# The down projection of a two-block layer as seven block products, with the next norm begun inside the last

## The chip, the cores and the metric

One core of one Trainium2 chip. The metric is the device time of the whole kernel in microseconds, the median of repeated runs of the same program with the same inputs (batch 1, 1024 tokens, width 1024, float32).

## The reference, cut to what matters

Two layers follow each other: a block with retention, forgetting attention and a gated feed-forward part, then a block with latent and dilated attention. The change touches the last product of the first block and the first norm of the second:

```python
h2 = rmsnorm(x, g_ffn)                                   # (1024, 1024)
ff = (silu(h2 @ w_gate) * (h2 @ w_up)) @ w_down          # hidden width D_FF = 2816 = 22 * 128
x = x + ff
# second block
h = rmsnorm_2(x, attn_norm_g)
proj = h @ w_in                                          # begins with c_q, c_kv, k_rope: 416 columns
```

All products must come out in near-float32 precision, so every operand is split.

## The kernel before

**Splitting.** Each operand `a` of a product is split into `ah` (rounded, by a copy) and `al = a - ah`, and a product is three matmuls, `ah bh + ah bl + al bh`, each of a 128x128 stationary tile and 512 moving columns, accumulated in a PSUM bank.

**Weights.** SyncE loads the weights of nearly all stages in units of 128x512 (256 KB) into the two slots of `raw` (L4131), in one long loop; GpSimd turns each unit into `wh` and `wl` (L4154, L4156) once the slot's last user has begun the next one. The eight units of the latent projection get tiles of their own (L2975, L2977), and GpSimd begins them when the down projection's splits stand at 18 of the second half's 22 (`COVERED`).

**The stage before.** `FeedForward` makes the hidden tensor: tile by tile, 22 tiles of 128 features by 1024 tokens. Its weights go through `up_raw`. Tiles 2 to 21 leave a two-slot staging area for `ff_dram` and come back into `FF` (11 MB in SBUF) by five loads (`BACK`, L2536) on ScalarE's DMA queue: the first (3 MB) while the last tiles are made, the other four (2, 1.5, 1.5 and 2 MB) at once after the last tile.

**`Down`.** `X += FF^T w_down`, in two halves `c` of 512 output columns. For each half it runs over the 22 feature tiles; per tile ScalarE copies it to `fh` (L2791, L2795, L2802, L2810), VectorE subtracts (`fl`, L2831, L2837, L2847, L2852), and TensorE does 8 token tiles x 3 matmuls of `fh`/`fl` with the unit's `wh`/`wl` (L2895), in all eight PSUM banks. That is 2 x 22 x 8 x 3 = 1056 matmuls. The four 1 MB loads of `X` from `x_dram` (L2813) are issued one per two tiles in the midst of the first half. VectorE adds the banks to `X` (L2859) after each half. The last two tiles of the second half (L2876) run staggered, so that the third norm begins beside them: squares and roots on ScalarE (L544, L570), scaling on VectorE (L613), transposes on TensorE (L667), a copy (L516) and a subtraction (L619) into `hth` and `htl`, the split operand of what follows. The norm does all of its token tiles in one order, with the transposes of tiles 0 and 1 inside the last product and those of tiles 2 and 3 behind it.

**The stage after.** `Latent` (L335) takes tokens 0 to 511 over eight 416-column units, with the transposes of tiles 4 to 7 between them, then tokens 512 to 1023.

Each engine runs its own list in program order. Lists are written out by hand; a wait stops all that stands behind it on its engine.

## Time and profile before

| | |
|---|---|
| median of 3 runs | 2978.2 us (2977.5 to 2980.61) |
| the profiled execution | 2988.91 us, its span 2987.1 us |
| mean granted TensorE clock | 0.983 |
| busy: TensorE, its weight loads | 2880.0 us, 2311.1 us |
| busy: VectorE, ScalarE, GpSimd | 1801.3 us, 1146.4 us, 823.0 us |
| DMA | 251.63 MB, 84 GB/s in the mean |

The profiled execution is 10.7 us longer than the median; all times of the trace are its own. The profile gives for each engine its busy time, and for each group of instructions what ended the idle time before it. Recorded matmuls overlap, so the time of one is read from the distance of starts, not from its duration. Times in the views below are microseconds from the start of the span.

### The profile page before, as it was taken

The numbers are of one execution on the slowest core, as the hardware profiler recorded it, in microseconds if no ns is written. First come the engines' busy times: TensorE is split into PE (matmuls) and PEld (weight loads), VectorE is DVE, ScalarE is ACT, GpSimd is POOL, SyncE is SP. The second block draws the span as 40 slices with busy tenths as digits, with TensorE's granted clock in tenths as the row PEclk, the third lists the DMA queues.
The fourth block names the chain that finished last, engine by engine and source line by source line (L and its number), as shares of the span: only waits on it lengthen the run. The fifth ranks groups of instructions, "written<-read, shape, count | busy, mean of one in ns | idle before, by whom it ended". The sixth has DMA issues, their size and how long they took to land.

```text
span 2987.1 us, 37403 instructions
## 1 busy us (share of the span) xinstructions
PE 2880.0 (96%) x14042; PEld 2311.1 (77%) x14042; DVE 1801.3 (60%) x2313; ACT 1146.4 (38%) x1908; POOL 823.0 (28%) x581
## 2 busy tenths in 40 slices
PE   7999999899999999999999999999999999999998
PEld 6778777678877888887888766668788888877886
DVE  2583666675587665554436488850566565686568
ACT  2232555433034333321223366641445444444313
POOL 2414110311532000004443600014344343440253
PEclk8999999999999999999999999999999999999999
DMA  3102000224433222225113300013323323223452
GB/s 131 39 22 83 18 22 22 74 85 151 169 120 116 99 85 71 78 102 186 60 46 112 99 8 15 22 41 103 95 74 82 80 72 82 68 78 113 155 192 97
DMA packets 112536, 251.63 MB, mean 84 GB/s; under 512 B 13441, under 2 KB 26497, under 8 KB 108289
## 3 DMA queue, kind: packets, MB, share of 16 engines
q1 hardware_dynamic: 64736, 131.91, 13.7%
q10 hardware_dynamic: 47648, 117.62, 11.7%
q8 instruction: 106, 1.74, 0.2%
q14 instruction: 46, 0.37, 0.0%
HBM read 184.48 MB, written 52.43 MB: 79 GB/s over the span
## 4 chain that ended last, share of the span: by engine, by line
PE 77%; DVE 13%; ACT 4%; issue 2%; POOL 1%; DMA 1%; ACTq 1%; POOLq 0%; SPq 0%; DVEq 0%
PE ps L390 13%; PE ps L2773 13%; PE ps L335 8%; PE ps L2895 8%; PE ps L1972 7%; PE ps L2002 6%; PE ps L2360 3%; PE ps L1172 3%; PE ps L1214 1%; PE ps L1189 1%; PE ps L3111 1%; PE ps L1191 1%; PE ps L3368 1%; PE ps L1190 1%; PE ps L374 1%
## 5 line engine op out<-in xcount | busy, mean ns | idle before, releaser
L4154 POOL TENSOR_TENSOR wh<-raw,zeros 128x512 fp32r<-128x512 f32 x276 | 324.8, 1177 | 2120.1 <-DMA raw<-in_stream_dram 627.2
L4156 POOL TENSOR_TENSOR wl<-raw,wh 128x512 fp32r<-128x512 f32 x276 | 463.0, 1677 | 21.7
L390 PE MATMUL ps<-hth,wh 128*128 128x512 f32 x704 | 286.3, 407 | 2.1 <-DVE fox_vl L1396 2.1
L390 PE MATMUL ps<-hth,wl 128*128 128x512 f32 x704 | 280.4, 398 | 0.0
L390 PE MATMUL ps<-htl,wh 128*128 128x512 f32 x704 | 280.1, 398 | 0.0
L2831 DVE TENSOR_TENSOR htl<-ff,hth 128x1024 fp32r<-128x1024 f32 x40 | 82.4, 2060 | 139.8 <-ACT hth L2802 71.0
L390 PEld LDWEIGHTS ps<-htl,wh 128*128 128x128 f32 x704 | 133.3, 189 | 32.4
L390 PEld LDWEIGHTS ps<-hth,wh 128*128 128x128 f32 x704 | 133.4, 189 | 31.9 <-issue 2.5
L390 PEld LDWEIGHTS ps<-hth,wl 128*128 128x128 f32 x704 | 133.8, 190 | 26.1
L2895 PE MATMUL ps<-wh,hth 128*128 128x512 f32 x336 | 133.0, 396 | 0.5 <-DVE htl L2837 0.5
L2895 PE MATMUL ps<-wh,htl 128*128 128x512 f32 x336 | 132.9, 396 | 0.0
L2895 PE MATMUL ps<-wl,hth 128*128 128x512 f32 x336 | 132.9, 395 | 0.0
L335 PE MATMUL ps<-wh,hth 128*128 128x512 f32 (+1 forms) x320 | 123.4, 386 | 4.5 <-POOL wl L4156 1.6
L2773 PE MATMUL ps<-htl,up_wh 128*128 128x512 f32 x320 | 126.1, 394 | 0.0
L2773 PE MATMUL ps<-hth,up_wh 128*128 128x512 f32 x320 | 126.1, 394 | 0.0
L2773 PE MATMUL ps<-hth,up_wl 128*128 128x512 f32 x320 | 126.1, 394 | 0.0
L1106 ACT ACTIVATE ps<-ps 128x512 f32<-128x512 f32 x224 | 122.8, 548 | 0.0
L335 PE MATMUL ps<-wl,hth 128*128 128x512 f32 (+1 forms) x320 | 121.7, 380 | 0.0
L335 PE MATMUL ps<-wh,htl 128*128 128x512 f32 (+1 forms) x320 | 121.3, 379 | 0.0
L1105 ACT ACTIVATE mla_pth<-ps 128x512 fp32r<-128x512 f32 x128 | 76.3, 596 | 80.4 <-PE ps L1172 78.9
L2540 ACT ACTIVATE up_wh<-up_sums 128x512 fp32r<-128x512 f32 x80 | 50.1, 631 | 143.9 <-PE ps L2773 133.0
L2002 PE MATMUL ps<-merge_oth,wh 128*128 128x512 f32 x256 | 102.1, 399 | 0.0
(603 smaller groups left out, 7691.5 us busy)
## 6 DMA issues: line engine op xcount, KB each, us to landing
raw<-in_stream_dram SPq DMA_DIRECT2D x284, 256.0 KB, 2.6
up_raw<-in_stream_dram SPq DMA_DIRECT2D x21, 1024.0 KB, 5.7
merge_raw<-in_stream_dram SPq DMA_DIRECT2D x12, 1024.0 KB, 7.1
merge_sg_dram<-merge_sg ACTq DMA_DIRECT2D x12, 1024.0 KB, 5.7
merge_sg<-merge_sg_dram ACTq DMA_DIRECT2D x12, 1024.0 KB, 4.9
dil_stg<-dil_stg ACTq DMA_DIRECT2D x96, 128.0 KB, 2.4
ff_dram<-ff SPq DMA_DIRECT2D x20, 512.0 KB, 3.0
merge_m<-in_stream_dram ACTq DMA_DIRECT2D x6, 1024.0 KB, 5.3
```

What stands on the lines that cost most here:

```text
L335: ins = nc.tensor.matmul(ps[:, t, 0:n], a[:, k, P * t:P * t + P], b[:, slot(j), c:c + n], start=first and q == 0, stop=final and q == 2)
L390: ins = nc.tensor.matmul(ps[:, bank + half, :], w[:, j, c:c + P], a[:, k, HALF * half:HALF * half + HALF], start=k == 0 and q == 0, stop=k ...
L1106: a.did(nc.scalar.activation(self.scores(g), self.scores(g), ACT.Exp, scale=self.scale), f"p{g}")
L1172: ins = nc.tensor.matmul(self.scores(g), m, r, start=q == 0, stop=q == len(pairs) - 1)
L1972: ins = nc.tensor.matmul(self.made(i, k), w[:, n, P * kt:P * kt + P], m[x][:, kt, :], start=begins and kt == 0 and q == 0, stop=kt == 3 an ...
L2002: ins = nc.tensor.matmul(ps[:, bank + half, :], w[:, br, P * k:P * k + P], x[:, 4 * br + k, HALF * half:HALF * half + HALF], start=n == 0 ...
L2360: ins = nc.tensor.matmul(ps[:, bank + t, :], xh[:, j, P * t:P * t + P], w, start=begins and q == 0, stop=ends and q == 2, skip_group_check ...
L2773: ins = nc.tensor.matmul(self.made(i, k), w[:, n, P * kt:P * kt + P], m[x][:, kt, :], start=begins and kt == 0 and q == 0, stop=kt == 3 an ...
L2831: nc.vector.tensor_tensor(self.fl[:, s, :], self.ff.FF[:, bass.ds(2 * i + s, 1), :].rearrange("p a b -> p (a b)"), self.fh[:, s, :], ALU.s ...
L2895: ins = nc.tensor.matmul(ps[:, t, :], a[:, s, P * t:P * t + P], b[:, s, :], start=first and q == 0, stop=final and q == 2)
L4154: nc.gpsimd.tensor_tensor(wh[:, s, :], raw[:, s, :], zeros[:].to_broadcast([P, HALF]), ALU.add).then_inc(w_hi, 1)
L4156: nc.gpsimd.tensor_tensor(wl[:, s, :], raw[:, s, :], wh[:, s, :], ALU.subtract).then_inc(w_split, 1)
```

## The change

The hidden tensor and the weights are taken as two by two blocks: P, Q (tokens 0 to 511, first and second half of the features) and R, S (tokens 512 to 1023), each of 11 feature tiles; the weights E, F (first half of the features by two column halves) and G, H. Seven products of blocks (11 feature tiles, 4 token tiles, 512 columns, 3 matmuls: 132 each) in this order, with S1 = R + S, S2 = S1 - P, S3 = S - R (all as `x_sum` or `s3`), S4 = Q - S2, and sums T of weight blocks (`w_sum`): `E_P`, `T_S1`, `T_S2`, `G_Q`, `T_S3`, `H_S4`, `T_S`. Each product runs in six steps, one tile and then five pairs of tiles; step n is product n // 6, step n % 6 of it; a full step is 24 matmuls. Products alternate between PSUM banks 4 to 7 and 0 to 3; two pairs of products are accumulated in one bank, and results are added to up to two places of `X`.

Weights no longer pass through the units of `raw` and GpSimd. SyncE loads them as 128x1024 (512 KB) into three slots, 48 loads in all since the sums read blocks again (two per step in `T_S1`); ScalarE copies (`weight_high`) and VectorE subtracts (`weight_low`) into a ring of three places in `wh`/`wl` and free parts of `hth`/`htl`; the hidden tiles have a ring of two (`hidden_high`, `hidden_low`). All sums are made on VectorE, in place, one step ahead. The four loads of `X` are issued right behind those of `FF`. The third norm takes tokens 0 to 511 inside the last product (squares after step 34, roots after 38; transposes of tile 0 after step 38, of 1 and 2 inside 39 and 40, of 3 after 40). GpSimd begins the latent units when all splits of `Down` are done. The core of the diff, `...` where lines are left out:

```diff
@@ class Down @@
+            ADDS = (((0, 0),), ((0, 1), (1, 1)), ((0, 1),), ((0, 0),), ((1, 1),), ((0, 1),), ((1, 0),))
...
+            def raw_released(self, eng, m):
+                if m < 6:
+                    eng.wait_ge(self.w_low, m + 1)
+                elif m < 18:
+                    eng.wait_ge(self.w_sums, (m - 6) // 2 + 1)
...
+            def weight_high(self, act, n):
+                k, g = divmod(n, self.GROUPS)
+                if n in (1, 2):
+                    self.ff.p.wait(act, f"u2x4.{PAIRED - 1}")
+                elif n:
+                    self.group_done(act, n - 3)
...
+                nc.scalar.activation(self.w_ring(n)[0], self.w_source(k, g), ACT.Copy).then_inc(self.w_high, 1)
+
+            def hidden_high(self, act, n):
...
+                    self.group_done(act, n - 2)
...
+            def first_highs(self, act):
+                self.weight_high(act, 0)
+                self.ff.v.wait(act, f"ff1.{PAIRED - 2}")
+                self.hidden_high(act, 0)
+                self.hidden_high(act, 1)
 
             def act(self, act, norm):
+                self.weight_high(act, 1)
                 self.ff.v.wait(act, f"ff2.{PAIRED - 1}")
...
                 for n in range(1, len(self.ff.BACK)):
                     self.ff.load_back(act, n)
...
+                for t in range(0, NT, 2):
+                    act.dma_start(self.X[:, t:t + 2, :], self.x_dram[:, t:t + 2, :]).then_inc(self.loaded, 16)
+                for n in range(2, self.LAST + 1):
+                    self.weight_high(act, n)
...
+                    self.hidden_high(act, n)
+                    if n == 34:
...
+                        norm.load(act)
+                        for t in range(4):
+                            norm.late_square(act, self.summed, t, 0)
+                    elif n == 38:
+                        norm.late_warm(act)
+                        for t in range(4):
+                            norm.late_root(act, self.summed, t)
...
+            def sums(self, dve, n):
...
+                if k == self.T_S1:
...
+                    self.x_sum(dve, R_, R_, S_, ALU.add)
+                    e = self.load_no(k, g, True)
+                    self.raw_loaded(dve, e - 1)
+                    self.raw_loaded(dve, e)
+                    self.w_sum(dve, T, raw, self.raw(e, g))
+                elif k == self.T_S2:
+                    dve.wait_ge(self.x_sums, g + 1)
+                    self.x_sum(dve, R_, R_, P_, ALU.subtract)
+                    self.raw_loaded(dve, self.load_no(k, g))
+                    dve.wait_ge(self.w_sums, g + 1)
+                    self.w_sum(dve, T, raw, T)
...
             def dve(self, dve, norm):
...
+                for n in range(2, self.LAST + 1):
+                    k, g = divmod(n, self.GROUPS)
+                    if n == 38:
+                        norm.late_base(dve, 0)
+                        for t in range(4):
+                            self.add(dve, self.H_S4, t)
+                    if n < self.LAST:
+                        self.sums(dve, n + 1)
+                    if k == self.T_S2:
+                        self.s3(dve, g)
+                    self.weight_low(dve, n)
...
+                    self.hidden_low(dve, n)
+                    if 0 < k < 6 and 2 <= g:
+                        self.add(dve, k - 1, g - 2)
+                    if n == 39:
+                        norm.scaled(dve, 0)
+                        norm.scaled(dve, 1)
...
+                    pe.wait_ge(self.w_low, n + 1)
+                    pe.wait_ge(self.x_low, n + 1)
+                    for j in range(self.size(g)):
+                        for t in (2, 3, 1, 0) if n == 0 else range(4):
+                            if g == 0:
+                                self.accumulator_free(pe, k, t)
+                            for q, (a, b) in enumerate(((xh, bh), (xh, bl), (xl, bh))):
+                                ins = nc.tensor.matmul(ps[:, self.BANK[k] + t, :], a[:, j, P * t:P * t + P], b[:, j, :], start=fresh and g == 0 and q == 0,
...
@@ class Latent @@
-                pool.wait_ge(down.hi, FT + self.COVERED)
-                pool.wait_ge(down.lo, FT + self.COVERED)
+                down.split_through(pool)
```

## Rows read from the trace of the kernel before

**Rows 1.** The page: busy time, share of the span, instructions of TensorE.

```profile
PE 2880.0 (96%) x14042; PEld 2311.1 (77%) x14042; DVE 1801.3 (60%) x2313; ACT 1146.4 (38%) x1908; POOL 823.0 (28%) x581
```

**Rows 2.** Stretches, the whole stage: us, busy time (count) by engine, PEclk, DMA share, GB/s.

```profile
1344.46:1602.39 257.93, 252.12 (x1090) 202.31 (x1088) 111.57 (x77) 61.00 (x84) 117.07 (x100) 0.99 0.30 102
```

**Rows 3.** Groups of instructions, 1344.46 to 1602.39: count | busy us, mean ns | idle before.

```profile
L2895 PE MATMUL ps<-wh,hth 128*128 128x512 f32 x336 | 133.0, 396 | 0.5 <-DVE htl L2837 0.5
L2831 DVE TENSOR_TENSOR htl<-ff,hth 128x1024 fp32r<-128x1024 f32 x40 | 82.4, 2060 | 139.8 <-ACT hth L2802 71.0 <-ACT hth L2810 68.9
L2810 ACT ACTIVATE hth<-ff 128x1024 fp32r<-128x1024 f32 x20 | 21.2, 1060 | 88.3 <-PE ps L2895 88.3
L2859 DVE TENSOR_TENSOR down_x<-down_x,ps 128x512 f32<-128x512 f32 x14 | 8.9, 678 | 1.0 <-PE ps L2876 1.0
L2975 POOL TENSOR_TENSOR lat_wh<-raw,zeros 128x416 fp32r<-128x416 f32 x7 | 8.6, 1230 | 1.8 <-DMA raw<-in_stream_dram 1.8
L667 PE MATMUL ps<-ident,norm_xn 128*128 128x128 f32 x32 | 5.1, 313 | 3.6 <-DVE norm_xn L613 3.6
```

**Rows 4.** Timeline of TensorE's weight loads: start us, us, engine, line, operands.

```profile
1330.17 0.19 PEld L2773 LDWEIGHTS ps<-up_x2h,up_wl 128*128 128x128 f32 x1
...
1335.61 0.19 PEld L2773 LDWEIGHTS ps<-up_x3h,up_wl 128*128 128x128 f32 x1
...
1569.89 0.19 PEld L2895 LDWEIGHTS ps<-wh,hth 128*128 128x128 f32 x1
...
1576.89 0.19 PEld L2895 LDWEIGHTS ps<-wh,hth 128*128 128x128 f32 x1
```

**Rows 5.** Timeline of TensorE, 1602 to 1611, same columns, idle time before in brackets.

```profile
1602.39 0.71 PE L335 MATMUL ps<-lat_wh,hth 128*128 128x416 f32 x1 [1.41 <-DVE htl L619]
1606.72 1.76 PE L667 MATMUL ps<-ident,norm_xn 128*128 128x128 f32 x8
1610.57 1.03 PE L667 MATMUL ps<-ident,norm_xn 128*128 128x128 f32 x8
```

**Rows 6.** Stretches elsewhere, columns as in rows 2.

```profile
855.00:865.00 10.00, 8.18 (x29) 6.28 (x28) 9.80 (x8) 2.12 (x3) 4.25 (x2) 0.83 0.46 173
1350.00:1360.00 10.00, 9.53 (x41) 7.36 (x41) 4.41 (x3) 2.12 (x2) 4.66 (x4) 1.00 1.01 392
1600.00:1610.00 10.00, 8.59 (x34) 7.87 (x33) 8.30 (x13) 5.16 (x13) 5.60 (x5) 0.59 0.48 158
```

**Rows 7.** Timeline of VectorE at both ends of the stage.

```profile
1349.64 1.23 DVE L2837 TENSOR_TENSOR htl<-ff,hth 128x1024 fp32r<-128x1024 f32 x1 [1.18 <-ACT hth L2795]
1590.69 1.28 DVE L613 SCALAR_TENSOR_TENSOR norm_xn<-down_x,norm_r,norm_g 128x1024 f32<-128x1024 f32 x1
1592.49 1.28 DVE L619 TENSOR_TENSOR htl<-ps,hth 128x512 fp32r<-128x512 f32 x2
```

**Rows 8.** Timeline of ScalarE's sequencer after the last hidden tile.

```profile
1348.63 2.02 ACTq L2536 DMA_DIRECT2D ff<-ff_dram  x4
```

**Rows 9.** Instructions of line 2813: ns min/median/max, first and last start us.

```profile
L2813 ACTq DMA_DIRECT2D down_x<-x_dram x4: 326/332/339, 1385.4 to 1418.9; - x4
```

**Rows 10.** DMA issues in 1350.1 to 1351: count, KB, us from issue to landing.

```profile
ff<-ff_dram ACTq DMA_DIRECT2D x1, 2048.0 KB, 23.1
```

**Rows 11.** DMA queues in 1357 to 1360: packets, MB, share of 16 engines.

```profile
q10 hardware_dynamic: 240, 0.96, 79.9%
q1 hardware_dynamic: 140, 0.26, 22.5%
```

**Rows 12.** DMA issues in 1348–1352, 1352–1357, 1367–1371, 1580–1583.

```profile
raw<-in_stream_dram SPq DMA_DIRECT2D x1, 256.0 KB, 2.7
raw<-in_stream_dram SPq DMA_DIRECT2D x1, 256.0 KB, 6.8
raw<-in_stream_dram SPq DMA_DIRECT2D x1, 256.0 KB, 3.1
norm_g<-in_attn_norm_g_dram ACTq DMA_DIRECT2D x1, 512.0 KB, 3.8
```

More of the change, by code:

```diff
@@ L2777, in build_two_blocks @@
         class Down:
-            TRANSPOSES = {4: 0, 6: 1}
+            E_P, T_S1, T_S2, G_Q, T_S3, H_S4, T_S = range(7)
+            GROUPS, LAST = 6, 7 * 6 - 1
+            BANK = (4, 0, 4, 0, 4, 0, 4)
+            FRESH = (0, 1, 3, 5)
+            ADDS = (((0, 0),), ((0, 1), (1, 1)), ((0, 1),), ((0, 0),), ((1, 1),), ((0, 1),), ((1, 0),))
             def __init__(self, scope, ff, x_dram):
                 self.ff, self.x_dram = ff, x_dram
-                self.fh, self.fl = hth[:, 4:6, :], htl[:, 4:6, :]
@@ new lines, in __init__ @@
+                self.raw_slots = (own[:], htl_f[:, 5:7, 0:HALF], htl_f[:, 3:5, 0:HALF])
+                self.raw_in = [sem(f"down_raw_in{n}") for n in range(3)]
+                self.x_sums, self.s3_made, self.w_sums = sem("down_x_sums"), sem("down_s3_made"), sem("down_w_sums")
+                self.x_high, self.w_high = sem("down_x_high"), sem("down_w_high")
+                self.x_low, self.w_low = sem("down_x_low"), sem("down_w_low")
+                self.done, self.full, self.added = sem("down_done"), sem("down_full"), sem("down_added")
@@ new lines, in raw, with raw_loaded, x_source, w_source @@
+            def raw(self, m, g):
+                return self.raw_slots[m % 3][:, 0:self.size(g), :]
+            def raw_loaded(self, eng, m):
+                eng.wait_ge(self.raw_in[m % 3], 16 * (m // 3 + 1))
+            def x_source(self, k, g):
+                return self.hidden(*((0, 0), (1, 0), (1, 0), (0, 1), (0, 0), (0, 1), (1, 1))[k], g)
+            def w_source(self, k, g):
+                if k in (self.T_S1, self.T_S2):
+                    return self.kept(g)
+                if k == self.T_S:
+                    return self.last_sum(g)
+                return self.raw(self.load_no(k, g), g)
@@ new lines, in added_at, with sp, load @@
+            def added_at(self, k, t):
+                return 4 * sum(len(x) for x in self.ADDS[:k]) + len(self.ADDS[k]) * (t + 1)
+            def sp(self, sp):
+                def load(m, half, c, g):
+                    if m in (1, 2):
+                        self.ff.p.wait(sp, f"g2c.{PAIRED - 1}")
+                    elif m:
+                        self.raw_released(sp, m - 3)
+                    sp.dma_start(self.raw(m, g), self.weights(half, c, g)).then_inc(self.raw_in[m % 3], 16)
+                for g in range(self.GROUPS):
+                    load(self.load_no(self.E_P, g), 0, 0, g)
+                for g in range(self.GROUPS):
+                    load(self.load_no(self.T_S1, g), 0, 1, g)
+                    load(self.load_no(self.T_S1, g, True), 0, 0, g)
+                for k, half, c in ((self.T_S2, 1, 1), (self.G_Q, 1, 0), (self.T_S3, 0, 0), (self.H_S4, 1, 1), (self.T_S, 1, 0)):
+                    for g in range(self.GROUPS):
+                        load(self.load_no(k, g), half, c, g)
@@ new lines, in weight_high @@
+            def weight_high(self, act, n):
[4 more added lines that the diff above has]
+                    self.group_done(act, n - 3)
+                if k in (self.E_P, self.G_Q, self.H_S4):
+                    self.raw_loaded(act, self.load_no(k, g))
+                else:
+                    act.wait_ge(self.w_sums, {self.T_S1: 0, self.T_S2: 6, self.T_S3: 12, self.T_S: 18}[k] + g + 1)
+                nc.scalar.activation(self.w_ring(n)[0], self.w_source(k, g), ACT.Copy).then_inc(self.w_high, 1)
@@ new lines, in hidden_high @@
+            def hidden_high(self, act, n):
+                k, g = divmod(n, self.GROUPS)
+                if n < 2:
+                    self.ff.p.wait(act, f"s4d.{PAIRED - 1}")
+                else:
+                    self.group_done(act, n - 2)
+                if k == self.E_P and g:
+                    act.wait_ge(self.ff.back[0 if g < 4 else 1], 16)
+                elif k == self.T_S3:
+                    act.wait_ge(self.s3_made, g + 1)
+                elif k in (self.T_S1, self.T_S2, self.H_S4):
+                    act.wait_ge(self.x_sums, {self.T_S1: 0, self.T_S2: 6, self.H_S4: 12}[k] + g + 1)
+                nc.scalar.activation(self.x_ring(n)[0], self.x_source(k, g), ACT.Copy).then_inc(self.x_high, 1)
```

358 lines of the change are left out of this document (195 added, 163 removed).

## The prediction

> **What bounds the kernel now.** First the page: TensorE is busy 96% of the 2987.1 us span, so the first question is how many matmuls go and at what price [rows 1]. Then the stretch that the change rewrites, from the first weight load of the down projection to the first matmul of the latent projection: 257.93 us, TensorE busy for 252.12, the granted clock 0.99, VectorE busy for only 111.57 [rows 2]. The groups of that stretch show who has room: the matmuls of L2895 (three groups of 336, of which one stands) wait 0.5 us in all, and 48 of L2876 close the product; VectorE's splits take 2060 ns each, with 139.8 us of idle time before them; half of ScalarE's copies take 1060 ns with 88.3 us before them [rows 3]. So this stage is bound by TensorE, and VectorE has some 146 us free. The period of one matmul is not its recorded 396 ns (they overlap): thirty weight loads lie between 1569.89 and 1576.89, so 0.2333 us each; in the stage before, with operands in other tiles, 24 took 5.44 us, 0.2267 each [rows 4].
>
> The budget closes: 1056 x 0.2333 = 246.4, four transposed tiles 5.1, idle time 0.5 + 3.6 + 1.4 before them and before the latent projection, together 257.0 of 257.9 [rows 2 to 5]. The clock stands at 0.59 in 1600 to 1610, after those idle times, that is partly at 1.2 instead of 2.4 GHz: the latent projection's first twelve matmuls and the eight transposes behind them take until 1608.5, 6.1 us; at full clock that is twelve of 0.19 (estimated from the tile, 416/512 of 0.2333) and 1.03, 3.3. That loses 2.8 us [rows 5, 6].
>
> **Matmuls removed.** Seven products of 11 x 4 x 3 = 132 are 924 against 1056: 132 x 0.2333 = 30.8 us less, 215.6 left. The splits' operands now sit in `wh` and `hth`, as at L2895, so I take 0.2333; at 0.2267 it were 6.1 us less again. Four tiles' transposes stay, 4 x 1.03 = 4.1 [rows 4, 5].
>
> **VectorE's price.** The splits of 128x1024 cost 2060 ns, but one outside GpSimd's weight splits took 1.23 us [rows 3, 7]. The change takes GpSimd out of this stage. Recorded times overlap too: two of 128x512, 0.68 each, end after 1.28, so the second costs 0.60; the same 0.09 off 1.23 leaves 1.14 for 128x1024 [rows 3, 7]. Per full step (24 matmuls, 5.6 us) VectorE does: in E_P and G_Q 2 instructions, in T_S3, H_S4 and T_S 3, in T_S1 4, in T_S2 5; adds of 0.6 come on top in the last four steps of each product. T_S1: 4 x 1.14 + 0.6 = 5.2, just under 5.6. T_S2: 5 x 1.14 + 2 x 0.6 = 6.9 in three steps, over by 1.3 each; with 1.3 in the small step and 0.1 in the next, 5.3 over. What VectorE can be ahead is little, because the ring for the hidden tile has two places: its copy starts when step n-2 is done, and 1.06 + 1.14 + 0.3 of hand-overs later the split is ready, 2.9 us before its turn. 5.3 - 2.9 = **2.4 us** of stall. ScalarE has 2 x 1.06 of 5.6 and covers that.
>
> **ScalarE's queue at the start.** Once the hidden tile 19 is made, ScalarE issues four loads of `FF` and, new, at once four of `X`, and only then copies for step 2. Four issues took 2.02 us; an `X` load occupies the sequencer 0.33, 0.45 with what lies between as I estimate, so about 3.9 us from 1348.6 [rows 8, 9]. Then come two copies and a split: 1352.5 + 2 x 1.06 + 1.14 + 0.2 = 1356.0, while step 1 ends at 1344.7 + 36 x 0.2333 = 1353.1. **3.0 us** (bounds 1 and 5: issues that cost nothing extra, or 1 us each). Before, the next copy was needed only at a step whose operands were there.
>
> **The weights' loads behind the burst.** Before, weights came in units of 256 KB, 2.7 us each, 6.8 while `FF` came back [rows 12]; they were asked for 11 us ahead and nobody waited. `FF`'s four loads landed one behind the other, the last 23.1 us after its issue at 1350.2, so at 1373.3, with the DMA engines at 1.01 and 392 GB/s [rows 6, 10]. The 4 MB of `X`, issued from 1385 to 1419 before [rows 9], now follow directly: another 10 to 13 us, so the burst lasts to about 1385. Within it, 140 packets of the weights' queue (128 carry a unit) ran in 1357 to 1360 beside 240 of ScalarE's: some 2.6 us per 256 KB, and 6.8 - 2.6 = 4.2 before the first [rows 11, 12]. Now follow the chain. T_S1 needs two loads per step. Those of its first step are released by the splits of steps 3 and 4, queue behind a 512 KB load that the split of step 2 releases at 1355, and land by 1355 + 4.2 + 4 x 2.6 = 1370, so step 5 just starts in time (1372.9). The loads of its second step wait for the split of step 5 (1371.6), are 512 KB each, and VectorE is to form that sum before it splits for the first step: 1371.6 + 4.2 + 4 x 2.6 = 1386.2, one sum of 1.14, two small splits of 0.6: step 6 starts at 1388.6, and step 5 ended at 1378.5. **10.0 us**. The load that the sum of step 8 needs is released by the sum of step 7 (1387.3), lands 4 us later behind its forerunner (512 KB outside a burst: 3.8 [rows 12]), then 3 x 1.14: 1395.0 against 1391.4, **3.6 us**. From there each sum has its load in 4 us of a 5.6 us step, and the stall ends. Bounds of the two together: 1 us (no burst: two loads in 5.4 us fit) and 16.
>
> A rule bears on this. The Trainium skill (DMA: Bandwidth & Descriptors, Queues, rings and completion order) says that each DMA engine takes turns between the queues that have work, packet by packet. The trace shows 140 against 240 packets, not even turns [rows 11]. By even turns the weights, with packets half as large, would get a third of the bandwidth, 1 MB in some 8 us instead of 10.4, and the time would be 2956.
>
> **The last product.** Tile 1's transposes wait for its scaling, which VectorE does behind the splits of step 39, whose copies stand behind four roots on ScalarE: **1.2 us**, estimated from 1.28 us for a scaling without GpSimd [rows 7] (bounds 0 and 4). The first four tiles then need nothing more at the end: the idle 3.6 and 1.4 us go [rows 3, 5], and the latent projection begins at full clock, 2.8 us saved. GpSimd starts its eight latent units only after the last split, but that is about 11 us before the end (two full steps less 2.6, two tiles' transposes), and a unit costs two instructions of 1.23 [rows 3], as much as its first twelve matmuls: covered; without that cover the latent projection would wait 3 us for its first unit. SyncE's loads for them stand behind the product's last weight load, which a sum releases some two steps before the end, early enough for the first two units. The latent stage's other half (tiles 4 to 7) is ordered as before.
>
> **Clock.** TensorE was idle for 1.8 us of 855 to 865, and the clock's mean fell to 0.83 there [rows 6], a loss of 1.7 us. The stall of 3 us is followed by one that absorbs a slow step, and so is that of 10 us. I count **1.0 us** (bounds 0 and 8, each stall followed by 1.7).
>
> **Sum.** 215.6 + 4.1 + 2.4 + 3.0 + 13.6 + 1.2 + 1.0 = 240.9 instead of 257.9: 17.0, and 2.8 from the clock, 19.8 us less. The profiled execution took 2988.9; 2969.1 after. The median of the three runs lies 10.7 lower, 2978.2, so the forecast is 2958.4, say **2959**.
>
> **Rivals.** (A) The weights are not late: the queue keeps its own pace, or the sums find their loads there. Then T_S1 costs 1 instead of 13.6: 2946; with 0.2267 per matmul 2940. For it: a load issued in 1367 to 1371, while `FF`'s last one was still under way, landed in 3.1 us. Against: the 6.8 in its midst [rows 12]. (B) Slower: VectorE's instructions keep the 2060 ns [rows 3], because not GpSimd but the tiles or the DMA writes make them slow. Then T_S1 takes 5.5 x 4 x 2.06 + 2.6 = 48 instead of 30.8, T_S2 62, the three products of three instructions about 37 each, some 65 us of stall beyond the sum less 5 that the burst hides: 3019. It decides from about 1.5 us per instruction: T_S1 and T_S2 hold 49.5 of them, and 19.8/49.5 = 0.4 above 1.14. Against it: the 1.23, measured while `FF`'s loads began [rows 7]. (C) The stalls bring the clock down each time, and VectorE's gaps are 0.1 larger than I took: 7 + 5 more, 2971. (D) The change saves nothing that can be told, since A's opposite and C come together (issues of 1 us, +2; the burst at 16, +2.4; C's 12): 2976.
>
> **How the numbers follow.** Forecast (2950 to 2966) 0.50; A 0.24; C 0.14; D 0.07; B 0.05. What this kernel's measurement can tell from no change is about 0.2%, 6 us. So faster 0.87, the same 0.07, slower 0.06. The range takes in A to its lower matmul price and C and D: 2940 to 2976.
>
> **What would show it.** Right: 924 matmuls at 0.233; no GpSimd in the stage; VectorE's 128x1024 at 1.2 us; TensorE waiting once about 3 us behind a ScalarE copy, then about 10 and 4 behind VectorE's splits while VectorE itself waits for a weights' DMA; short waits in T_S2; no idle between the last product and the latent projection. Wrong: a gain of over 30 us says that the burst doesn't reach the weights; VectorE at 2 us says B; a latent projection that waits for GpSimd says that its start is not covered.

## The result

| | before | changed | ratio, 95% interval |
|---|---|---|---|
| median, four runs each | 2979.14 us (2977.5 to 2980.61) | 2958.84 us (2954.28 to 2966.69) | 0.9919 (0.9903 to 0.9935) |
| profiled execution, its span | 2988.91 us, 2987.1 us | 2966.69 us, 2964.8 us | |
| first Down matmul to first latent matmul | 257.7 us | 238.1 us | |
| from there to the end | 1384.7 us | 1380.4 us | |

The change makes the kernel 20.3 us faster; 19.8 was forecast, 2959. The total is right and its terms are not: three of them miss by 8.5, 8.6 and 3.9 us, in both directions, and cancel. (In the profiled executions the stage goes from 1344.69 to 1602.39 of 2987.1 before, and from 1346.32 to 1584.43 of 2964.8 after. The forecast counted it from the first weight load, 0.2 us earlier.)

The page's line on TensorE and the stage as one stretch, which answer to [rows 1, 2]; the columns are the same:

```profile
PE 2845.7 (96%) x13910; PEld 2284.8 (77%) x13910; DVE 1856.8 (63%) x2418; ACT 1178.5 (40%) x1948; POOL 723.6 (24%) x493
```

```profile
1346.32:1584.43 238.11, 219.88 (x957) 178.29 (x956) 170.09 (x181) 91.99 (x124) 5.85 (x6) 0.97 0.43 156
```

132 matmuls are gone from the kernel (13910 for 14042). But where TensorE was busy for all but 5.8 us of the stage, it now stands still for 18.2, GpSimd has left the stage, and VectorE works 170 us instead of 112. The groups say who the new waits are owed to, and that VectorE's price is the one that was forecast ([rows 3] had 2060 ns):

```profile
L3100 PE MATMUL ps<-hth 128*128 128x512 f32 x224 | 89.3, 399 | 15.8 <-DVE htl L2960 15.7
L2960 DVE TENSOR_TENSOR htl<-ff,hth 128x1024 fp32r<-128x1024 f32 x35 | 42.7, 1221 | 33.7 <-ACT hth L2894 33.7
L3100 PE MATMUL ps<-wh,hth 128*128 128x512 f32 x84 | 33.5, 399 | 2.5 <-DVE wl L2954 1.3 <-DVE htl L2960 1.2
```

L2954 and L2960 are the splits of weights and hidden tile, L3100 is the matmul. TensorE's timeline places these waits (idle time before in brackets): before step 2, step 6, step 7, and twice in `T_S2`, before steps 15 and 16. A first matmul behind a wait that is recorded at 0.76 instead of 0.47 us is at half clock (1.2 instead of 2.4 GHz).

```profile
1366.12 0.76 PE L3100 MATMUL ps<-hth 128*128 128x512 f32 x1 [11.37 <-DVE htl L2960]
...
1391.33 0.47 PE L3100 MATMUL ps<-wh,hth 128*128 128x512 f32 x1 [1.27 <-DVE wl L2954]
...
1397.64 0.77 PE L3100 MATMUL ps<-hth 128*128 128x512 f32 x1 [3.28 <-DVE htl L2960]
...
1441.70 0.47 PE L3100 MATMUL ps<-wh,hth 128*128 128x512 f32 x1 [1.18 <-DVE htl L2960]
...
1448.57 0.47 PE L3100 MATMUL ps<-hth 128*128 128x512 f32 x1 [1.04 <-DVE htl L2960]
```

**The wait of 11.4 us.** It stands where the prediction put one of 3.0, behind VectorE and ScalarE. ScalarE's timeline, its sequencer as ACTq:

```profile
1350.13 2.15 ACTq L2498 DMA_DIRECT2D ff<-ff_dram  x4
1352.30 10.12 ACTq L2909 DMA_DIRECT2D down_x<-x_dram  x4
1362.53 1.06 ACT L2880 ACTIVATE hth<-htl_f 128x1024 fp32r<-128x1024 f32 x1 [14.89 <-issue]
```

`FF`'s four loads are issued in 2.15 us, as before. The four of `X` behind them take 10.12 us, the first alone 6.50 (1352.30 to 1358.80), the others 1.07 to 1.25; before the change one took 0.33 [rows 9]. The sequencer stands in the DMA instruction itself, and the copy for step 2 stands behind it: "issue" is idle time for which the profile shows no releaser, and here it is the mark of the trouble.

**The waits at steps 6 and 7.** VectorE's timeline there (L2975 is `w_sum`, L2972 `x_sum`):

```profile
1380.56 1.22 DVE L2954 TENSOR_TENSOR htl<-htl_f,hth 128x1024 fp32r<-128x1024 f32 x1
1381.69 1.22 DVE L2960 TENSOR_TENSOR htl<-ff,hth 128x1024 fp32r<-128x1024 f32 x1
1382.83 1.22 DVE L2972 TENSOR_TENSOR ff<-ff 128x1024 f32<-128x1024 f32 x1
1388.80 1.23 DVE L2975 TENSOR_TENSOR hth_f<-htl_f,down_raw 128x1024 f32<-128x1024 f32 x1 [4.75 <-DMA down_raw<-in_stream_dram]
1389.94 0.69 DVE L2954 TENSOR_TENSOR wl<-htl_f,wh 128x512 fp32r<-128x512 f32 x1
1390.54 0.68 DVE L2960 TENSOR_TENSOR htl<-ff,hth 128x512 fp32r<-128x512 f32 x1
```

VectorE waits 4.75 us for a weights' load, to form the sum of step 7, and the two small splits of step 6, whose operands have been there for long, stand behind it. TensorE starts step 6 at 1391.33, 1.4 us late. The mechanism is the one forecast, the 10.0 us aren't there: step 5 began at 1384.5, not at 1372.9 (1.6 of this only because the whole stage began later on this trace's clock), so most of the lateness of the loads is hidden behind that of step 2.

### The profile page after: what moved, and what is told of

It is laid out like the page before. It is cut to its first block, busy times and chain, and to the rows that moved or that the text cites. A ratio compares the mean times of both kernels' runs of the same rounds, so it can differ in the third digit from the quotient of the medians.

```text
span 2964.8 us, 36741 instructions
## 1 busy us (share of the span) xinstructions
PE 2845.7 (96%) x13910; PEld 2284.8 (77%) x13910; DVE 1856.8 (63%) x2418; ACT 1178.5 (40%) x1948; POOL 723.6 (24%) x493
## 3 DMA queue, kind: packets, MB, share of 16 engines
q10 hardware_dynamic: 47648, 117.62, 11.7%
## 4 chain that ended last, share of the span: by engine, by line
PE 76%; DVE 14%; ACT 4%; issue 2%; DMA 1%; POOL 1%; ACTq 1%; POOLq 0%; SPq 0%; DVEq 0%
PE ps L394 13%; PE ps L2737 13%; PE ps L339 8%; PE ps L1934 7%; PE ps L1964 6%; PE ps L3100 5%; PE ps L2322 3%; PE ps L1134 3%; PE ps L3309 1%; PE ps L1176 1%; PE ps L1151 1%; PE ps L3566 1%; PE ps L1153 1%; PE ps L1152 1%; PE ps L378 1%
## 5 line engine op out<-in xcount | busy, mean ns | idle before, releaser
L4353 POOL TENSOR_TENSOR wh<-raw,zeros 128x512 fp32r<-128x512 f32 x232 | 286.1, 1233 | 1554.9 <-PE ps L394 563.9
L4355 POOL TENSOR_TENSOR wl<-raw,wh 128x512 fp32r<-128x512 f32 x232 | 405.0, 1746 | 18.2
L3173 POOL TENSOR_TENSOR lat_wh<-raw,zeros 128x416 fp32r<-128x416 f32 x8 | 7.4, 924 | 649.5 <-DVE htl L2960 644.8
L3974 DVE TENSOR_TENSOR dil_stg<-dil_stg,dil_cos 128x1024 f32<-128x1024 f32 x24 | 31.3, 1304 | 118.3 <-ACT dil_stg L3847 118.1
L3100 PE MATMUL ps<-hth 128*128 128x512 f32 x224 | 89.3, 399 | 15.8 <-DVE htl L2960 15.7
L1105 DVE TENSOR_TENSOR mla_ptl<-ps,mla_pth 128x512 fp32r<-128x512 f32 x128 | 87.7, 685 | 22.6 <-ACT ps L1068 21.7
```

Of the source, the lines that this page charges most:

```text
L1105: v.did(nc.vector.tensor_tensor(self.PTl[:, g % self.RING, at:HALF], self.scores(g), self.PTh[:, g % self.RING, at:HALF], ALU.subtract), f ...
L3100: ins = nc.tensor.matmul(ps[:, self.BANK[k] + t, :], a[:, j, P * t:P * t + P], b[:, j, :], start=fresh and g == 0 and q == 0, stop=final a ...
L4353: nc.gpsimd.tensor_tensor(wh[:, s, :], raw[:, s, :], zeros[:].to_broadcast([P, HALF]), ALU.add).then_inc(w_hi, 1)
L4355: nc.gpsimd.tensor_tensor(wl[:, s, :], raw[:, s, :], wh[:, s, :], ALU.subtract).then_inc(w_split, 1)
```

## Experiments

The kernel before ran in each group of runs on the same chip, with medians of 2985.3, 2983.95 and 2981.83 us; ratios are to it. "Stage" is the time from the first Down matmul to the first latent one in the profiled execution; it is the sharper measure, because the start of the stage, after work that is the same in all these kernels, lay anywhere from 1334.8 to 1346.3 us. Waits are the distance of two matmuls' starts less the usual one, some 0.15 more than the bracket.

| run | ratio (95%) | stage | main waits of TensorE before steps |
|---|---|---|---|
| the change | 0.9919 (0.9903 to 0.9935) | 238.1 | 2: 11.5; 6: 1.4; 7: 3.4; 15, 16: 1.3, 1.2 |
| a0 | 0.9925 (0.9909 to 0.9942) | 238.5 | 2: 11.9; 6: 0.5; 7: 3.9; 15, 16: 1.3, 1.2 |
| e1 | 0.9918 (0.9902 to 0.9935) | 235.0 | 2: 1.4; 6: 11.1; 7: 1.1; 15, 16: 1.3, 1.2 |
| e2 | 0.9915 (0.9899 to 0.9932) | 236.7 | 2: 1.7; 6: 7.9; 7: 3.6; 15, 16: 1.3, 1.2 |
| e3 | one run, 2961.62 us | 237.2 | 2: 11.8; 7: 3.7; 15, 16: 1.3, 1.2 |
| e7 | 0.9923 (0.9906 to 0.9941) | 236.4 | 2: 1.5; 6: 6.7; 7: 4.0; 13: 1.6; 15, 16: 1.3, 1.2 |
| e4 | 0.9912 (0.9895 to 0.9928) | 236.2 | 2: 12.5; 6: 2.4; 7: 2.8; none at 15, 16 |
| e5 | 0.9953 (0.9936 to 0.9971) | 246.2 | 2: 12.0; 6: 0.4; 7: 3.8; 15, 16: 1.3, 1.2; behind step 41: below |
| e8 | 0.9883 (0.9858 to 0.9907) | 226.7 | 7: 8.8 |
| e9 | 0.9915 (0.9897 to 0.9934) | 239.7 | 2: 11.7; 10: 4.2; 15, 16: 1.3, 1.2 |
| e10 | 0.9909 (0.9890 to 0.9929) | 233.7 | 8: 4.8; 10: 8.3 |
| e11 | 0.9898 (0.9880 to 0.9917) | 232.6 | 9: 5.2; 10: 7.3 |
| e12 | 0.9981 (0.9968 to 0.9994) | 258.9 | 2: 12.4; 6: 1.6; 7: 3.9; 12: 0.7; 13: 7.1; 14: 1.5; 15: 5.5 |

### The changed kernel once more, and X's loads moved (a0, e1, e2, e3)

The theories behind the prediction's two largest uncertain terms: the order of ScalarE's queue makes step 2 late, and the burst of loads makes the weights late.

> The changed kernel itself, once more, beside the variants on the same chip. Its first trace showed TensorE waiting 11.5 us before step 2 (forecast 3.0), 1.4 before step 6 (forecast 10.0), 3.4 before step 7 (forecast 3.6) and 2.6 in T_S2. Theory Q (ScalarE's queue): its sequencer is held at the first load of X, 6.5 us, and 14.9 us pass between two copies; the late step 2 then hides most of the wait for weights. Both theories expect 2959 here (2954 to 2967) and the same waits, so this run shows how far they repeat.

It repeats: 11.9 us before step 2, and TensorE stands still for 18.1 us of the stage, 18.2 in the first trace.

In e1 the four `X` loads leave the place behind `FF`'s, and one each stands behind the hidden copy of steps 3 to 6:

```diff
-                for t in range(0, NT, 2):
-                    act.dma_start(self.X[:, t:t + 2, :], self.x_dram[:, t:t + 2, :]).then_inc(self.loaded, 16)
...
                     self.hidden_high(act, n)
+                    if 3 <= n < 7:
+                        t = 2 * (n - 3)
+                        act.dma_start(self.X[:, t:t + 2, :], self.x_dram[:, t:t + 2, :]).then_inc(self.loaded, 16)
```

> The four loads of X are issued one each behind the hidden copies of steps 3 to 6, no longer in a row behind those of FF. The sequencer is held no more, but the loads still run directly behind FF's and beside the weights. Theory Q alone: step 2 waits 0 to 1 us instead of 11.5, the clock stays up (1.9 us), nothing comes back: 13 us less than the changed kernel, 2946. Theory B as well (the burst slows the weights, as I forecast): the waits before steps 6 and 7 grow from 1.4 and 3.4 to some 10 and 4, so about 8 of the 13 us come back: 2954.

The wait before step 2 falls from 11.9 to 1.4, so the order of that queue is its cause. Only 3.5 us of stage are gained, though, since TensorE now waits before step 6 (its timeline):

```profile
1387.40 0.77 PE L3101 MATMUL ps<-wh,hth 128*128 128x512 f32 x1 [10.96 <-DVE wl L2955]
```

That is the 10.0 us of the prediction, to within one. Its three weights' loads, 512 KB each, were issued at 1368.4 to 1369.3 and landed at 1378.7, 1384.8 and 1387.5. The expectation of 2954 was too good: 2960.75 was measured, which the medians can't tell from the changed kernel. Nor was the sequencer free, as had been expected: the first issue of `X`, at 1353.03, still took 3.90 us, but it stands behind the copies that steps 2 and 3 need.

In e2 the same loads stand behind the copies of steps 5 to 8.

> The same with the loads of X behind the hidden copies of steps 5 to 8, when FF's are nearly through; VectorE needs X in step 8. Theory Q alone: like the variant with steps 3 to 6, 2946. Theory B as well: now the weights of T_S1's second step meet one load of 1 MB at a time, the waits before steps 6 and 7 stay under 2 and 4 us, and this one is faster than that variant by about 6 us: 2946 against 2954. If X is too late for VectorE's first add, step 9 waits 1 to 3 us.

Step 6 waits 7.9 us instead of 11.1, but step 7 3.6; 2946 was expected and 2957.18 measured. Moving `X` alone isn't enough: `FF`'s own four loads, 7 MB, are under way until about 1371.

In e3 `X`'s loads are issued first and `FF`'s behind them.

> The four loads of X (1 MB each) are issued ahead of the four of FF (7 MB), all in a row as in the changed kernel. Theory Q1 (the queue holds the sequencer at the fifth DMA under way): the first FF load is the one that is held, some 6 us. Theory Q2 (it holds it by the packets under way: there were 7 MB in packets of 4 KB when X's first was held): four loads of 1 MB leave room for two of FF, and the third or fourth of them is held. In both the copies of step 2 come late by 6 us or more, and step 4 waits for FF in addition: 2 to 8 us slower than the changed kernel.

The wait before step 2 is 11.8 us, from the same place; the fear that step 4 would come late for want of `FF` was wrong. What the run gives is who is held. ScalarE's sequencer there:

```profile
1347.09 1.85 ACTq L2907 DMA_DIRECT2D down_x<-x_dram  x4
1349.03 10.58 ACTq L2498 DMA_DIRECT2D ff<-ff_dram  x4
1359.71 1.06 ACT L2880 ACTIVATE hth<-htl_f 128x1024 fp32r<-128x1024 f32 x1 [15.12 <-issue]
```

The issues of `X` now take 0.33 to 0.53 us; of `FF`'s four (2, 1.5, 1.5 and 2 MB) the first take 0.70 and 1.09, the last two 3.55 and 4.96. In the changed kernel the fifth issue was the first to be held, with 7 MB ahead of it; here it is the seventh, with 7.5 MB ahead. So it is not the kind of load and not the count of DMAs. The packets of that queue in the traces tell more: a packet is 4 KB of `FF` or 8 KB of `X`, and ahead of the load that was being issued there were, at the end of the four `X` issues of the changed kernel, 1252, 1252, 1267 and 1265 packets left, but 4.9, 5.4, 5.9 and 6.4 MB. In a0 it is 1218 to 1233 packets, in e1 1205 and in e3 1190 and 1309. Packets fit and bytes don't: with some 1200 to 1300 ahead the issue ends, and each further `X` load then takes the 1.1 to 1.25 us in which about as many packets drain as the 128 that it adds.

### The place of X's loads, later still (e7)

Behind the copies of steps 6 to 9; the four additions that need them stand two each in steps 10 and 11.

> The changed kernel with its four X loads one each behind the hidden copies of steps 6 to 9 (the additions that need them stand in steps 10 and 11, two in each). Two theories on the wait before step 6, which was 11.1 us with the X loads behind steps 3 to 6 and 7.9 with them behind steps 5 to 8. Theory B (bandwidth: the weights of steps 6 and 7 land late because 1 MB loads run beside them, FF's own four as well as X's): with X out of the way the FF loads alone are left, they land until some 1371 us on the span's clock, and the wait before step 6 is 3 to 6 us, that before step 7 under 3.6, and the time 2 to 4 us below the run with steps 5 to 8. Theory R (ring: those weights are asked for late, when their ring's places come free, and land late whatever runs beside them): the waits before steps 6 and 7 stay at 7.9 and 3.6 us.

6.7 us before step 6, 4.0 before step 7, and a new 1.6 before step 13: between the two theories, and no gain over e2. The first issue of `X` comes at 1368.64 here, behind those of all three weights' loads that steps 6 and 7 wait for (1365.45 to 1366.38), while `FF`'s last load is under way until 1374.2. So most of the lateness stays without `X` ahead of them, and `FF` is the likely cause; e8 tests it.

### All loads spread (e8)

```diff
-                for n in range(1, len(self.ff.BACK)):
-                    self.ff.load_back(act, n)
-                for t in range(0, NT, 2):
-                    act.dma_start(self.X[:, t:t + 2, :], self.x_dram[:, t:t + 2, :]).then_inc(self.loaded, 16)
+                self.ff.load_back(act, 1)
...
+                    if n in (2, 4, 6):
+                        self.ff.load_back(act, 1 + n // 2)
+                    if 7 <= n < 11:
+                        t = 2 * (n - 7)
+                        act.dma_start(self.X[:, t:t + 2, :], self.x_dram[:, t:t + 2, :]).then_inc(self.loaded, 16)
```

with the additions as in e7, and the sums `s3` as in e4, below.

> The changed kernel with FF's loads spread too: the first behind step 1's place as now, the second to fourth behind the hidden copies of steps 2, 4 and 6, X's four behind those of steps 7 to 10, the additions in later steps, and T_S2's sums of the latent in G_Q's steps. Theory B: never more than two loads of 1 MB are under way beside the weights, so no wait before step 2 over 2 us, none before step 6 over 1 us, and at step 7 at most the 3.5 us that it had; the stage from the first Down matmul to the first latent one takes 222 to 228 us against 238, and the whole 2945 to 2950 where before has 2979 (ratio near 0.989). Theory R: the waits before steps 6 and 7 together stay at 9 us or more, and the stage at 232 us or more.

2945.46 us, a ratio of 0.9883: the best of all runs, though its interval just reaches that of the change, since one of its four runs took 2955.68. Its stage is 11.4 us shorter; some 2 of these belong to the sums `s3` (e4). The stage as one stretch, and the one long wait on TensorE's timeline:

```profile
1335.53:1562.23 226.70, 217.84 (x957) 177.79 (x956) 169.99 (x181) 92.63 (x123) 5.85 (x6) 0.98 0.47 164
```

```profile
1377.37 0.77 PE L3105 MATMUL ps<-hth 128*128 128x512 f32 x1 [8.64 <-DVE htl L2962]
```

No DMA issue is held (all take 0.33 to 0.38 us), and steps 2 and 6 start on time; so theory B holds for them. For step 7 it was too bold, 8.8 us instead of 3.5. VectorE there:

```profile
1363.14 1.23 DVE L2977 TENSOR_TENSOR hth_f<-htl_f,down_raw 128x1024 f32<-128x1024 f32 x1 [3.61 <-DMA down_raw<-in_stream_dram]
...
1373.72 1.23 DVE L2977 TENSOR_TENSOR hth_f<-htl_f 128x1024 f32<-128x1024 f32 x1 [7.02 <-DMA htl_f<-in_stream_dram]
1374.87 1.22 DVE L2956 TENSOR_TENSOR htl<-hth_f,hth 128x1024 fp32r<-128x1024 f32 x1
1376.00 1.22 DVE L2962 TENSOR_TENSOR htl<-ff,hth 128x1024 fp32r<-128x1024 f32 x1
```

Step 7's own sum is formed at 1363.14. What VectorE waits 7 us for at 1373.72 is the sum of step 8, and step 7's splits are queued behind it.

### VectorE's order (e9, e10, e11)

In steps 5 to 9 the splits go first and the next step's sum behind them; e9 is the changed kernel with it, e10 is e8 with it, e11 is e10 with `FF`'s last load and `X`'s four one step later.

```diff
-                    if n < self.LAST:
+                    if n < self.LAST and not 5 <= n <= 9:
                         self.sums(dve, n + 1)
...
                     self.hidden_low(dve, n)
+                    if 5 <= n <= 9:
+                        self.sums(dve, n + 1)
```

> The changed kernel with one order on VectorE turned round: in steps 5 to 9 it splits for the step itself first and forms the sum for the next step afterwards, not the sum first. Theory V (what TensorE waits for before steps 6 and 7 is not that the weights of its own step are late, but that VectorE stands at the sum of the step behind, whose load is late, with this step's splits queued behind it): the waits of 1.4 us before step 6 and 3.4 before step 7 fall to 0.3 or less together, no wait over 0.5 comes before step 8, and with the half clock that follows them the time is 5 to 6.5 us below the changed kernel's. Theory L (the loads set the pace whatever VectorE's order is): the wait before step 6 goes and as much comes before step 7 or 8, and the time stays within 1.5 us of the changed kernel's. The wait of some 11.5 us before step 2 is the same in both.

> The kernel with all loads spread (2945.5 where before had 2984) with the same order on VectorE as in the run before: splits first, then the next step's sum, in steps 5 to 9. Its only long wait was 8.8 us before step 7, while the sum of step 7 itself had been formed 14 us earlier and that of step 8 stood on VectorE, waiting for a load. Theory V: step 7 starts at once, and step 8 waits 2.5 to 4 us for its own sum (load landed 1373.6 on that run's clock, then 1.23 + 1.06 + 1.22 of sum, copy and split against an end of step 7 at 1374.1). The time falls by 4 to 7 us, to a ratio of about 0.986. Theory L: the 8.8 us come before step 8 instead, and the time stays.

> As the run before, with FF's last load one step later (behind the hidden copy of step 7), X's four behind those of steps 8 to 11, and the four additions that need them all in step 11. If bandwidth is what is short between steps 5 and 8 (1 MB and 2 MB loads beside 512 KB ones that took 9.3 us instead of 3.8), the wait before step 8 falls from 2.5 to 4 us to under 1.5, and the time by a further 1 to 3 us. If X now lands too late for the additions, a wait of 1 to 5 us comes before step 12, and nothing is gained.

Each wait goes from where it was, and comes back. In e9 steps 6 and 7 start on time, and TensorE waits 4.2 us before step 10; in e10 it waits 4.8 before step 8, somewhat over the 2.5 to 4 expected, and then 8.3 before step 10, which nobody expected; in e11 the wait before step 8 is gone and none comes before step 12, but it has 5.2 before step 9 and 7.3 before step 10. e9 equals the changed kernel. e10 and e11 have longer stages than e8 (233.7 and 232.6 against 226.7); their medians are higher too (2955.21 and 2952.0 against 2945.46), but the intervals of the ratios overlap. The place before step 10 is my own seam: from step 10 on the old order holds again, so VectorE has two sums to form ahead of step 10's splits, and the second one's load is asked for only when the first is done. VectorE in e9:

```profile
1399.21 1.22 DVE L2975 TENSOR_TENSOR hth_f<-htl_f,down_raw 128x1024 f32<-128x1024 f32 x1
...
1404.58 1.23 DVE L2975 TENSOR_TENSOR htl_f<-htl_f 128x1024 f32<-128x1024 f32 x1 [2.42 <-DMA htl_f<-in_stream_dram]
1405.73 1.22 DVE L2954 TENSOR_TENSOR htl<-hth_f,hth 128x1024 fp32r<-128x1024 f32 x1
1406.86 1.22 DVE L2960 TENSOR_TENSOR htl<-ff,hth 128x1024 fp32r<-128x1024 f32 x1
```

So theory V is right on what TensorE stood behind before steps 6 and 7, and the time came out as theory L said. Whether that is because the loads set the pace, or only because of the seam, these runs don't show: the other order held through the whole stage was not tried.

### T_S2's work on VectorE (e4)

The sums `s3` stand in `G_Q`'s steps:

```diff
-                    if k == self.T_S2:
+                    if k == self.G_Q:
                         self.s3(dve, g)
```

> The changed kernel with one part moved: the sums of the latent of T_S2's steps (two of 0.6 us in each step) stand in G_Q's steps, so that VectorE has 5 x 1.14 = 5.7 us in a step of T_S2 against TensorE's 5.44 to 5.6, and 4 x 1.14 + 1.2 = 5.8 us in one of G_Q. If VectorE's time in T_S2's steps is what TensorE waits for (1.34 us before step 15, 1.21 before step 16), both waits fall to 0.2 or less each and the time is some 2.3 us below the changed kernel's (ratio to before near 0.9912 where the changed kernel has 0.992). If the waits come from ScalarE's copies or from a ring's free place instead, they stay where they are and the time is the changed kernel's.

Both waits are gone, so VectorE's load in those steps was their cause. The stage is 1.9 to 2.3 us shorter than the change's and a0's; the median, 2957.76, agrees with the 2.3 us forecast but can't prove it, since the intervals overlap.

### The norm inside the last product (e5)

The transposes, high and low parts of tiles 0 to 3 stand behind the last product.

> The changed kernel with the third norm's part undone: the transposes, high and low parts of tiles 0 to 3 stand behind the last product, as in the kernel before, and not within it. If this part is worth what the trace of before shows in front of the latent matmul (idle times of 3.6 and 1.4 us, and a granted clock at half for some time behind them, 2.8 us), the stage from the first Down matmul to the first latent one grows by 1 to 5 us and the whole by 5 to 9 us against the changed kernel. If the clock's dip in the latent stage comes whether TensorE stands still there or not, only the idle times come back and the whole grows by 2 to 5 us, with the latent stage as long as in the changed kernel.

The stage grows by 7.7 us against a0, the part behind it by 2.7 (1383.5 against 1380.8), the ratio from 0.9925 to 0.9953. TensorE behind the product, and a window across the start of the latent projection:

```profile
1574.77 1.91 PE L629 MATMUL ps<-ident,norm_xn 128*128 128x128 f32 x16
1579.38 1.48 PE L629 MATMUL ps<-ident,norm_xn 128*128 128x128 f32 x8 [2.71 <-DVE norm_xn L602]
1582.35 1.97 PE L629 MATMUL ps<-ident,norm_xn 128*128 128x128 f32 x8 [1.48 <-DVE norm_xn L602]
1585.73 0.71 PE L339 MATMUL ps<-lat_wh,hth 128*128 128x416 f32 x1 [1.41 <-DVE htl L608]
```

```profile
1585.00:1595.00 10.00, 8.69 (x41) 7.88 (x42) 7.62 (x14) 6.62 (x20) 1.96 (x2) 0.74 0.48 159
```

Idle time of 5.6 us, and the clock at half into the latent projection: the first of the two theories, and more than it said, 7.7 us of stage for the 1 to 5 expected. The whole is 10.4 us longer by the trace (7.7 + 2.7) and 8.7 by the medians of two groups (2970.51 against 2961.8); 5 to 9 was expected. The idle time is little more than the 3.6 and 1.4 us of [rows 3, 5]; most of the rest of the 7.7 us is transposes at half clock, 1.48 and 1.97 us for eight where 1.03 is usual. So this small part of the change is worth 10.4 us of the trace. In the changed kernel the clock holds from the first latent matmul on:

```profile
1584.43:1590.00 5.57, 5.57 (x35) 5.43 (x34) 5.35 (x10) 2.98 (x9) 4.17 (x4) 1.00 0.42 143
```

### GpSimd beside VectorE (e12)

The rival B was that something other than GpSimd made VectorE's splits slow. Here GpSimd gets empty work during `T_S2`:

```diff
+                pool.wait_ge(self.w_low, 6 * self.T_S2)
+                for i in range(24):
+                    if i:
+                        pool.wait_ge(self.beside, i)
+                    nc.gpsimd.tensor_tensor(raw[:, i % 2, :], raw[:, i % 2, :], zeros[:].to_broadcast([P, HALF]), ALU.add).then_inc(self.beside, 1)
```

> The changed kernel with work added that computes nothing new: from the start of T_S2 on GpSimd adds zeros to its two 128x512 unit tiles, which nobody reads then, 24 times in all. Theory P (GpSimd's access to the tiles is what made VectorE's splits take 2.06 us before the change): as long as GpSimd works, VectorE's 128x1024 instructions take about 2.06 us instead of 1.22, its five of them and two small ones per step fill 11 to 12 us where TensorE needs 5.5, and TensorE waits about half of GpSimd's time, 12 to 25 us more in all; outside that stretch the splits stay at 1.22. The rival (the place of the operands in the kernel before made them slow): they stay at 1.22 us beside GpSimd too, and the time doesn't change.

GpSimd worked from 1416.95 to 1460.21. Groups of 1425.13 to 1460.21, first its own, then two of VectorE's:

```profile
L3072 POOL TENSOR_TENSOR raw<-raw,zeros 128x512 f32<-128x512 f32 x19 | 33.7, 1772 | 1.5
```

```profile
L2962 DVE TENSOR_TENSOR htl<-ff,hth 128x1024 fp32r<-128x1024 f32 x3 | 6.2, 2056 | 0.0
...
L3026 DVE TENSOR_TENSOR down_x<-down_x,ps 128x512 f32<-128x512 f32 x4 | 2.5, 674 | 0.0
```

and of 1470 to 1560, without it:

```profile
L2962 DVE TENSOR_TENSOR htl<-ff,hth 128x1024 fp32r<-128x1024 f32 x16 | 19.6, 1225 | 24.2 <-ACT hth L2896 24.2
```

2056 ns beside GpSimd, the 2060 of [rows 3] almost exactly, and 1225 without. The ratio goes to 0.9981; the stage is 20.4 us longer than a0's, within the 12 to 25 expected; about 5.5 of it is half clock behind the waits before steps 13 and 15. Theory P stands. 43 us of GpSimd's work beside `T_S2` cost 20 us of stage, two thirds of the 30.8 of the removed matmuls, so the gain needs GpSimd out at least where VectorE is fullest. VectorE's additions, with one operand in PSUM, take 674 ns beside GpSimd and 681 without (1470 to 1560). The Trainium skill (SBUF — State Buffer, section "SBUF: two separate sides") says that VectorE contends with a GpSimd instruction that reads SBUF only where it reads two SBUF inputs itself (or is in a two-port mode); both rows agree with that.

## The prediction, point by point

| term | forecast | measured | |
|---|---|---|---|
| 924 matmuls | 215.6 | 211.7 | 0.2291 each in the mean, where the clock is full |
| transposes of four tiles | 4.1 | 3.6 | 0.92 and 3 x 0.79 on starts, and the matmul behind each 0.08 later |
| `T_S2` on VectorE | 2.4 | 2.6 | e4 takes it away |
| ScalarE's queue before step 2 | 3.0 | 11.5 | bounds were 1 and 5 |
| late weights, steps 6 and 7 | 10.0 + 3.6 | 1.4 + 3.4 | 11.1 + 1.1 in e1 |
| the last product | 1.2 | 0.2 | before step 38; tile 1's transposes wait for nothing |
| clock in the stage | 1.0 | 3.3 | 1.8 behind step 2's wait, 1.5 behind step 7's |
| small waits, the rest | | 0.4 | |
| sum | 240.9 | 238.1 | the rest is what the others leave |

**The failed step is that of ScalarE's queue.** It priced eight issues at what single ones had cost, 0.33 to 0.5 us [rows 8, 9]. Each of those stood in an emptier queue: `FF`'s four had nothing large ahead, and `X`'s came 35 us and more later, one at a time. The upper bound of 1 us per issue had no row of a full queue behind it. With 7 MB, 1786 packets, ahead, one issue took 6.5 us, until 1252 were left, and the next three 3.5 together. The trace of before couldn't show this price. A bound that it did allow is the drain of what is added: 4 MB at the 392 GB/s of [rows 6], 10.7 us. The 10.12 measured lie near it, but their mechanism is the packets above, so the nearness is partly chance.

**Late weights: mechanism right, size hidden.** The 10.0 us before step 6 assumed that step 5 ends at 1378.5. It ended at 1389.9, 11.4 us later: 8.5 by step 2's wait, 1.8 by the half clock behind it, 1.6 because the stage began later on this clock, less 0.5 for cheaper matmuls. Then the loads were nearly in time: 1.4. e1, where step 2 is on time, shows 11.1. The two terms are not additive; the loads are asked for when splits and sums free their slots, but a wait of one cause covers that of the other. That is the main reason why the total came out right, and it is luck: 3.0 + 10.0 forecast, 11.5 + 1.4 found. The matmuls' 3.9 us too much and the clock's 2.3 too little cancel in part as well. Step 7's 3.6 was 3.4.

**The rule on turns.** The prediction held that 140 packets against 240 [rows 11] speak against the Trainium skill's rule of turns packet by packet (DMA: Bandwidth & Descriptors, section "Queues, rings and completion order"). Queues in the trace of after, 1365 to 1369, right behind the issue of a weights' load at 1364.87, then 1369.5 to 1373.5:

```profile
q10 hardware_dynamic: 396, 1.56, 97.6%
q1 hardware_dynamic: 34, 0.07, 4.5%
```

```profile
q10 hardware_dynamic: 250, 1.16, 72.6%
q1 hardware_dynamic: 251, 0.48, 31.7%
```

For 3.6 us nothing, then 250 against 251: even turns, once the queue has something to send. In the trace of before the first packet of the load issued at 1354.08 came 3.5 us later, at 1357.56, not after the 4.2 that I took, so 1357 to 1360 began ahead of it; from 1358 to 1359.5 it is 95 against 102. So the rule agrees with the trace and my reading of the row was wrong; whether a turn is one of the profile's packets or several, these counts don't tell. What the turns share is packets and not bytes, and the weights' are the smaller ones: 0.48 MB against 1.16 here. In 1374 to 1378, beside `X`, it is 181 packets, 0.34 MB, against 180 with 1.31. The time by even turns would have been 2956, also within the measured runs; what it had right or wrong is hidden by the same cancelling.

**Matmuls.** 0.2333 was taken since the operands sit in `wh` and `hth`. The ring of weights has three places, and the weight loads' timeline shows that only one of them is at that price:

```profile
1467.56 0.19 PEld L3100 LDWEIGHTS ps<-hth 128*128 128x128 f32 x1
...
1473.00 0.19 PEld L3100 LDWEIGHTS ps<-wh,hth 128*128 128x128 f32 x1
...
1478.59 0.19 PEld L3100 LDWEIGHTS ps<-hth 128*128 128x128 f32 x1
```

Step 20 (weights in `hth`): 5.44/24 = 0.2267. Step 21 (in `wh`): 5.60/24 = 0.2333. Step 22 has its weights in the other place of `hth` and a mean of 0.2277, but this is no third price: its first five matmuls come every 0.232 and the rest, in the same tiles, every 0.2267. So the place is not all. The prediction named the lower price and 6.1 us for it, as part of rival A; 3.9 came.

**Clock.** After the 11.4 us the granted clock was down to half, and matmuls came 0.427 apart until 1369.7. The stretch 1360 to 1370, with 6 us of standing still in it:

```profile
1360.00:1370.00 10.00, 3.88 (x10) 3.09 (x11) 5.76 (x5) 4.84 (x5) 0.00 (x0) 0.51 1.03 410
```

3.3 us against 1.0, within its bounds of 0 and 8. Whether later waits absorbed a part of it, as the prediction claimed, these runs don't tell. The 2.8 us at the latent projection came as forecast: the part behind the stage is 4.3 us shorter than before, and 2.7 us longer again in e5. The other 1.5 lie within what this part differs by from run to run (1378.6 to 1380.8 us with the norm's part unchanged). No wait for GpSimd came at the latent projection: its first matmul follows the product's last by 0.23 us.

**Rivals.** B is refuted by the 1221 ns and, causally, by e12. A's condition, weights not late, didn't hold: 1.4 and 3.4 us here, 11.1 in e1. C's repeated loss of clock is half right, 3.3 instead of 1.0. D, no change that can be told, is excluded by the interval.

## What to carry to other kernels

A list of DMA issues on a compute engine's queue costs what an issue shows only as long as little is under way on it; with some 1300 packets ahead or more (5 MB of 4 KB ones), price the next issue by the time in which the queue drains, and keep the engine's copies ahead of it. Waits with different causes in one chain don't add: price each with the others present and with them absent, for undoing the first one may give back only what the second one was hiding, as 10.5 us at step 2 gave 3.5 of stage in e1. What helped is to spread all the loads over the steps that need them (e8: 11.4 us of stage, some 2 of them by `s3`), not to move one group of them.

## What the runs showed of the hardware beyond the forecast

- A DMA issue on ScalarE's queue took 0.33 us, and 6.5 with 1786 packets (7 MB) under way ahead of it; held issues ended with 1190 to 1309 packets left ahead of them, whatever the bytes (the change, a0, e1, e3).
- A 512 KB load needed 3.8 us alone [rows 12], 8.7 beside a saturated other queue, 3.6 of them before its first packet moved (1.0 for the load issued at 1348.92, with nothing beside it), and up to 18.1 in e1 with two more loads ahead of it and 1 MB loads beside it.
- Two queues that both have work share packets evenly: 251 of 2 KB to 250 of 4.6 KB in the mean, 181 to 180 of 7.3 KB.
- One and the same matmul comes every 0.2267 or 0.2333 us. The slower price goes with weights in `wh`, and in most steps behind such a one the first five to ten matmuls come almost as slowly (0.23; the step's mean is 0.2277 to 0.2288). No run here tells why.
